# Modulation weights of a two-layer encoder: moved into the projection stage, through more buffers

## The reference

```python
def rwkv7_time_mix(h, prev_x, prev_wkv, p, l):
    shifted = jnp.concatenate([prev_x[:, None, :], h[:, :-1]], axis=1)
    xm = h[:, :, None, :] + (shifted - h)[:, :, None, :] * p['rw_mu'][l]
    rkv = jnp.einsum('bsnd,nde->bsne', xm[:, :, :3], p['rw_w_rkv'][l])      # the projection stage
    ...
    kk = kk * lax.rsqrt(jnp.maximum(jnp.sum(kk * kk, axis=-1, keepdims=True), 1e-24))
    ...
def run_trunk(x, c, ...):
    cs = jax.nn.silu(c)
    for l in range(DEPTH):
        mod = cs @ p['ada_w'][l] + p['ada_b'][l]                            # (1024) @ (1024, 6144)
        sh1, sc1, g1, sh2, sc2, g2 = jnp.split(mod, 6, axis=-1)
        ...
        h = modulate(rmsnorm(x, g), sh1, sc1); x = x + g1 * mixer(h)
        h = modulate(rmsnorm(x, g), sh2, sc2); x = x + g2 * hier_moe(h, p, l)
# shared_kv: one more such product, silu(c) @ kv_ada_w, (1024) @ (1024, 2048)
```

## Time and profile before

| | |
|---|---|
| Time, median of 3 runs | 1529.16 us |
| Lowest, highest | 1525.72 us, 1533.57 us |
| The profiled execution, span | 1526.5 us |
| TensorE (PE) busy | 1355.7 us, 89% of the span |
| VectorE (DVE) busy | 521.2 us, 34% |
| ScalarE (ACT) busy | 361.9 us, 24% |
| Read from HBM | 293.73 MB, mean 194 GB/s |

### The profile page before, as it was taken

One profiled execution on the slowest core, in us unless ns is written; L12 is line 12 of the kernel. 1 busy time (PEld: TensorE's weight loads), 2 busy tenths in 40 slices (PEclk: granted clock), 3 DMA queues, 4 the chain that ended last, 5 costly groups with the idle time before them and its releaser, 6 DMA issues.

```text
span 1526.5 us, 27571 instructions
## 1 busy us (share of the span) xinstructions
PE 1355.7 (89%) x11807; PEld 822.6 (54%) x11807; DVE 521.2 (34%) x1268; ACT 361.9 (24%) x664; POOL 68.4 (4%) x77
## 2 busy tenths in 40 slices
PE   5699998888888968999999996987968999999994
PEld 2257665565675655554444444656755555444443
DVE  2503553333312452332223235143262333222324
ACT  1131301110122022222222222134132222222212
POOL 2000000000000010000000000000010000000000
PEclk9799989998999875999999997996965999999997
DMA  9333216766734320888888845050220888888830
GB/s 272 92 111 120 100 62 244 285 234 237 276 113 165 111 83 1 331 324 299 305 304 299 305 186 184 11 205 17 83 83 1 331 330 320 302 307 298 302 121 34
DMA packets 111383, 297.16 MB, mean 195 GB/s; under 512 B 5924, under 2 KB 7304, under 8 KB 104136
## 3 DMA queue, kind: packets, MB, share of 16 engines
q1 hardware_dynamic: 109248, 289.78, 51.7%
q0 software_dynamic: 1856, 6.15, 1.7%
q10 hardware_dynamic: 200, 0.06, 0.0%
HBM read 293.73 MB, written 2.24 MB: 194 GB/s over the span
## 4 chain that ended last, share of the span: by engine, by line
PE 81%; DMA 8%; DVE 7%; ACT 2%; issue 1%; SPq 0%; DVEq 0%; POOL 0%; ACTq 0%; POOLq 0%
PE bank L664 79%; DMA ring<-in_ada_w 7%; DVE work L1415 3%; DMA ring<-in_kv_ada_w 1%; ACT work L1173 1%; PE bank L992 1%; DVE x_res L1421 1%; DVE work L1418 1%; DVE rstd L1453 1%; DVE att L1814 0%; PE bank L1159 0%; PE bank L1129 0%; PE bank L682 0%; SPq L450 0%; DVE work L1421 0%
## 5 line engine op out<-in xcount | busy, mean ns | idle before, releaser
L664 PE MATMUL bank<-work 128*128 128x128 bf16 (+6 forms) x3936 | 385.2, 255 | 20.0 <-ACT work L1173 7.4
L664 PEld LDWEIGHTS bank<-work 128*128 128x128 bf16 (+2 forms) x3936 | 282.1, 110 | 132.5 <-issue 30.6
L664 PE MATMUL bank<-ring,work 128*64 128x512 f32 (+1 forms) x1760 | 351.4, 553 | 1.5 <-DVE ring L1415 1.5
L664 PE MATMUL bank<-work,ring 128*128 128x320 f32 (+4 forms) x1600 | 298.9, 362 | 11.5 <-DVE work L1418 7.0
L664 PEld LDWEIGHTS bank<-work,ring 128*128 128x128 f32 (+3 forms) x1600 | 215.7, 171 | 96.2 <-issue 23.9
L664 PEld LDWEIGHTS bank<-ring,work 128*64 128x64 f32 (+1 forms) x1760 | 116.9, 138 | 214.1 <-issue 193.5
L664 PE MATMUL bank<-ring 64*64 64x64 f32 (+2 forms) x2624 | 110.7, 231 | 5.0 <-issue 5.0
L664 PEld LDWEIGHTS bank<-ring 64*64 64x64 f32 (+2 forms) x2624 | 97.5, 143 | 31.3 <-issue 25.1
L1173 ACT ACTIVATE work<-bank 64x512 f32<-64x512 f32 (+7 forms) x110 | 52.9, 528 | 226.1 <-PE bank L664 176.9
L664 PE MATMUL bank<-ring,cs 128*32 128x512 f32 x448 | 64.7, 671 | 38.6 <-DMA ring<-in_ada_w 34.4
L1762 DVE TENSOR_TENSOR work<-work,bank 128x320 f32<-128x320 f32 x128 | 62.4, 487 | 95.3 <-PE bank L664 95.3
(11 more groups left out here) (167 smaller groups left out, 879.9 us busy)
## 6 DMA issues: line engine op xcount, KB each, us to landing
ring<-in_moe_w_gu SPq DMA_DIRECT2D x64, 2048.0 KB, 12.9
ring<-in_moe_w_down SPq DMA_DIRECT2D x64, 1024.0 KB, 12.3
ring<-in_ada_w SPq DMA_DIRECT2D x40, 1024.0 KB, 5.1
ring<-in_rw_w_rkv SPq DMA_DIRECT2D x6, 2048.0 KB, 8.0
ring<-in_ada_w SPq DMA_DIRECT2D x4, 2048.0 KB, 31.5
ring<-in_kv_ada_w SPq DMA_DIRECT2D x8, 1024.0 KB, 5.0
ring<-in_rw_w_o SPq DMA_DIRECT2D x2, 2048.0 KB, 11.7
ring<-in_at_w_q SPq DMA_DIRECT2D x2, 2048.0 KB, 14.8
```

The lines of the kernel that those rows point to most:

```text
L664: return eng.matmul(out, l, r, start=start, stop=stop, **kw)
```

## The change

24 of the 48 steps move into the projection stage, one after each of its 24 output blocks (`project` gets an argument `step`). The chunk loop keeps two steps per chunk, and each level four, one after j = 0, 1, 2 and 4; as 48 steps are used up, level 5 has only two and level 6 none. Three buffers are used at first (steps 0 to 14), two for steps 15 to 23, three others from step 24 on (one of them shared). The weight loads of the projection are put between the pieces in SyncE's queue. Some small tiles move: `shiftT` and `modrow[0]` get places that are free in the projection stage, the load of `swin` waits for the last piece in its place, ScalarE waits for the shift output before it writes over `shiftT`, and for step 14 before it writes `vb` over a buffer. The two calls of `project` for n = 2 get `step=2 * C`, and the chunk loop on every engine goes over `steps_of_chunk(j)`.

```diff
-A_STEPS = 4
-LEVEL_STEPS = (2, 0, 2, 0, 2)
+P_STEPS = 24
+A_STEPS = 2
+LEVEL_STEPS = (1, 1, 1, 0, 1)
-    first = A_STEPS * NCH + sum(LEVEL_STEPS) * (l - 2)
+    first = P_STEPS + A_STEPS * NCH + sum(LEVEL_STEPS) * (l - 2)
+def steps_of_chunk(j):
+    return range(P_STEPS + A_STEPS * j, P_STEPS + A_STEPS * (j + 1))
+def mod_place(n):
+    if n < 15:
+        return n % 3
+    if n < P_STEPS:
+        return (n - 15) % 2
+    return (1, 3, 4)[(n - P_STEPS) % 3]
+def mod_before(n):
+    return max((k for k in range(n) if mod_place(k) == mod_place(n)), default=None)
+def mod_last(b):
+    return max(k for k in range(MSTEPS) if mod_place(k) == b)
...
-        shiftT = ring[:, tail1 + 1536:tail1 + 1792]
-        mw = [ring[:, 3 * B:3 * B + 2048], ring[:, tail3:tail3 + 2048]]
-        modrow = [ring[:, 3 * B + 2048:3 * B + 2560], work[:, 6 * B:6 * B + 512]]
+        shiftT = work[:, 7 * B:7 * B + 256]
+        mw = [ring[:, 4096:SLOT], ring[:, tail1:tail1 + 2048], work[:, 5 * B:5 * B + 2048],
+              ring[:, 3 * B:3 * B + 2048], ring[:, tail3:tail3 + 2048]]
+        modrow = [state[:, 1].rearrange("p c k -> p (c k)"), work[:, 6 * B:6 * B + 512]]
...
@@ SyncE's queue @@
-            for n in (1, 0, 2):
-                for hf in range(2):
-                    half(("rkv", n, hf), i["rw_w_rkv"][0, n], hf)
-            for n in range(MSTEPS):
+            def mod_load(n):
                 ...
-                if n >= 2:
-                    sp.wait("mod used", n - 2)
-                elif n == 1:
+                if mod_before(n) is not None:
+                    sp.wait("mod used", mod_before(n))
+                if n == P_STEPS + 1:
+                    sp.wait("used", "rkv", 2, 1)
+                if n == P_STEPS + 2:
                     sp.wait("bonus all", C - 1)
                 ...
+            for n in range(3):
+                mod_load(n)
+            for hf in range(2):
+                half(("rkv", 1, hf), i["rw_w_rkv"][0, 1], hf)
+            halves = {6: (0, 0), 10: (0, 1), 14: (2, 0), 17: (2, 1)}
+            for n in range(3, MSTEPS):
+                if n in halves:
+                    m, hf = halves[n]
+                    half(("rkv", m, hf), i["rw_w_rkv"][0, m], hf)
+                mod_load(n)
...
@@ GpSimd @@
-            pl.wait("wkv ready")
+            pl.wait("mod used", mod_last(1))
             eng.dma_start(swin, ...)
...
@@ TensorE @@
-            def project(tag, outs, src, wname, ready=None):
+            def project(tag, outs, src, wname, ready=None, step=None):
                     pe.did(ins, *keys)
+                    if step is not None:
+                        mod_step(step + m)
...
-                project(("rkv", n), range(C), xm[n], lambda hf, n=n: ("rkv", n, hf), ("xm", n))
+                project(("rkv", n), range(C), xm[n], lambda hf, n=n: ("rkv", n, hf), ("xm", n), step=C - C * n)
...
...
@@ ScalarE @@
             projected(1, kb, range(C))
+            mod_copy(range(0, C))
...
+            eng.wait_ge(in_sems["out_written"], 32)
             projected(0, rr, range(C))
+            mod_copy(range(C, 2 * C))
...
+            ac.wait("mod used", mod_last(2))
             projected(2, vb, range(4))
...
             projected(2, vb, range(4, C))
+            mod_copy(range(2 * C, 3 * C))
...
@@ VectorE @@
             ve.wait("xm used", 0)
+            mods_out(range(0, 2 * C))
...
             op(eng.tensor_copy(dend[:, :, :], dec[:, :, CH - 1:T:CH]))
+            mods_out(range(2 * C, 3 * C))
...
+            ve.wait("mod used", mod_last(0))
             for j in range(NCH):
```

More of the change, by code:

```diff
@@ L540, in _ @@
                 (ring[0:32, SLOT + 3072:SLOT + 4096], i["rw_g2"][0, P:LG])])
-            for n in (1, 0, 2):
-                for hf in range(2):
-                    half(("rkv", n, hf), i["rw_w_rkv"][0, n], hf)
-            for n in range(MSTEPS):
+            def mod_load(n):
                 w, l, blk, _b = MODS[n // C]
                 src = i[w] if l is None else i[w][l]
-                if n >= 2:
-                    sp.wait("mod used", n - 2)
-                elif n == 1:
-                    sp.wait("bonus all", C - 1)
-                else:
-                    sp.wait("used", "rkv", 2, 1)
-                eng.dma_start(mw[n % 2], src[P * (n % C):P * (n % C) + P, 2048 * blk:2048 * (blk + 1)]
-                              ).then_inc(in_sems[f"modw_in{n % 2}"], 16)
+                if mod_before(n) is not None:
[3 more added lines that the diff above has]
+                if n == P_STEPS + 2:
+                    sp.wait("bonus all", C - 1)
+                eng.dma_start(mw[mod_place(n)], src[P * (n % C):P * (n % C) + P, 2048 * blk:2048 * (blk + 1)]
+                              ).then_inc(in_sems[f"modw_in{mod_place(n)}"], 16)
+            for n in range(3):
[8 more added lines that the diff above has]
+                mod_load(n)
             sp.wait("mod used", MSTEPS - 1)
@@ L692, in mod_step @@
                         bank.hold("mod", g)
-                    eng.wait_ge(in_sems[f"modw_in{n % 2}"], 16 * (n // 2 + 1))
-                    pe.did(mod_rows(ps[seen_bank(("mod", g))], c, mw[n % 2]), ("mod used", n), ("mod", g))
+                    b = mod_place(n)
+                    eng.wait_ge(in_sems[f"modw_in{b}"], 16 * sum(mod_place(k) == b for k in range(n + 1)))
+                    pe.did(mod_rows(ps[seen_bank(("mod", g))], c, mw[b]), ("mod used", n), ("mod", g))
                 elif n == MSTEPS:
@@ L800, in _ @@
             head_sums("kk sum", nrm)
-            project(("rkv", 2), range(4), xm[2], lambda hf: ("rkv", 2, hf), ("xm", 2))
+            project(("rkv", 2), range(4), xm[2], lambda hf: ("rkv", 2, hf), ("xm", 2), step=2 * C)
             pe.wait("kk rstd")
@@ L805, in _ @@
             head_sums("bonus sum", tmp)
-            project(("rkv", 2), range(4, C), xm[2], lambda hf: ("rkv", 2, hf))
+            project(("rkv", 2), range(4, C), xm[2], lambda hf: ("rkv", 2, hf), step=2 * C)
             seen.at[("xm used", 2)] = (pe.name, pe.n)
@@ L832, in _ @@
                         full(ins, "A" + nm, j, hf)
-                for n in range(A_STEPS * j, A_STEPS * j + A_STEPS // 2):
+                for n in steps_of_chunk(j)[:A_STEPS // 2]:
                     mod_step(n)
@@ L843, in _ @@
                     full(ins, "tok" + nm, j)
-                for n in range(A_STEPS * j + A_STEPS // 2, A_STEPS * (j + 1)):
+                for n in steps_of_chunk(j)[A_STEPS // 2:]:
                     mod_step(n)
@@ L1249, in _ @@
                         ("read", "tok" + nm, j), ("tok ready", j))
-                mod_copy(range(A_STEPS * j, A_STEPS * (j + 1)))
+                mod_copy(steps_of_chunk(j))
             for l in range(2, 7):
@@ L1575, in _ @@
                 tt_(nl[:, :, t], nt[:, :, t], bmid(wcst("lev")[:, 64:128], C), M, ("level", 2, j))
-                mods_out(range(A_STEPS * j, A_STEPS * (j + 1)))
+                mods_out(steps_of_chunk(j))
                 ve.settle()
```

3 lines of the change are left out of this document (2 added, 1 removed).

## The result

The changed kernel takes 1492.21 us, the median of four runs (1489.34 to 1493.97), against 1527.44 us for the kernel before, measured beside it (four runs, 1520.86 to 1533.57). The ratio is 0.9759, with a 95% interval from 0.9725 to 0.9793. The forecast was 1491 us. The profiled execution has a span of 1492.2 us; it is the longest of the four, and its time was 1493.97 us.

A forecast was written before the change was run, and what follows sets the result against it. TensorE, 81% of the chain, was held in the loops by late weights and slow clock. Steps +4.1, waits -28.2 and clock -13.7 gave -37.8 on 1526.5, so 1488.7; plus 2.7, 1491 us (8 in 10: 1482 to 1506).

The forecast's parts named there:

- Waits for weights: Chunk and level loops: TensorE's 28.2 us of waits for modulation weights go, with 0 new waits taken.
- Clock: Chunk and level loops: 13.7 us of slow clock go back to the waits and vanish with them; at least 0.
- the work at full clock: Chunk and level loops without waits at full clock, all 48 steps included: 156.1 us, where the stretch took 202.3.
- Rival 2: Chunk and level loops: the waits go but the clock stays low, +13.7 us, 1505 us; chance 0.12.
- Steps in the projection: Projection stage: 24 added steps cost 1.15 us each, +27.6 us; bounds 0.93 to 1.61 each.
- Rival 1: Projection stage: each step drains the array, 1.61 us per step, +11 us, 1502 us; chance 0.13.
- an unseen cost per change of shape: Steps among full-array projection matmuls: a cost per array-shape change that no row shows, named the likeliest error; no size given.
- Steps out of the loops: Chunk and level loops: 24 steps leave, at 0.98 us each, -23.5 us.
- rival 3: Projection stage: DMA does not keep up and waits move there, ending slower, near 1550 us at 180 GB/s; chance 0.04.
- the milder form of this rival: Projection stage: at 240 GB/s DMA, steps 10, 14 and 17 wait some 9 us; 1500 us.
- Rival 4: Loops: they wait on something else, such as VectorE in the levels, turning 28 us of waits into others; chance 0.03.
- New waits: 0 new weight waits, at worst a few us; other engines cost nothing except up to 1 us for VectorE in level 6.

The follow-up runs named there:

- two_buffers_new_place: The changed kernel with two buffers at any time instead of three; 1492.48 us, ratio 0.9777.
- pieces_not_reloaded: The kernel before with only the first two weight pieces loaded and multiplied again by later steps, so results are wrong; 1481.95 us, ratio 0.9697.
- the two traffic kernels: The kernel before with weight loading kept up but no step waiting for it, in steady half-size or dense whole transfers; 1512.41 and 1486.14 us.
- pairs_in_projection: The changed kernel with two steps after every second projection block instead of one after each; 1486.99 us, ratio 0.9727.
- half pieces: The kernel before with three buffers and all steps in the old place, each piece loaded as two transfers of 1024 columns; 1510.44 us, ratio 0.9857.

## Why the prediction was right

It was right in the time (1491 against 1492.21 us), in both halves of the sum, and in their causes. That it came within 1.2 us is partly luck. It forecast a fall of 37.8 us; the medians fell by 35.2 and the profiled spans by 34.3. It started from a median of 1529.16 us for the kernel before, and the four runs beside the result have 1527.44, which hides 1.7 us of the difference. By its own terms:

- **Waits for weights, -28.2: right.** 28.2 before, none after. The cause was put down to supply in the chunks and spacing in the levels. `two_buffers_new_place` shows that the place is what does it: with half of the traffic gone from the loops, two buffers are enough.
- **Clock, -13.7: right in size, though the term holds more than clock.** `pieces_not_reloaded` gives back all 16.7, and the two traffic kernels show that it hung on the waits and not on the traffic. Apart from the first chunk's `A` groups the slow rows come to 12.3 us; some 4 us are the overlap lost at the waits, which the sum did not know. It did not show, as the work at full clock was put too high: 156.1 us, where `pieces_not_reloaded` has 153.8 without its slow `A` groups. 3.0 were set aside for those groups (6.61 us); in the changed kernel they take 5.38, so part of that came too. Rival 2, the clock staying low, falls: 0.97 and 1.00 in the loops.
- **Steps in the projection, +27.6 at 1.15 each: right.** A block and its step take 5.50 us where a block alone took 69.17 / 16 = 4.32: 1.18 a step, +28.3. With two turns (0.53 each) and a wait of 0.47, and 0.4 less elsewhere, that is the stretch's 29.4. Rival 1, the full drain at 1.61, falls: the price of a change there and back is 0.33 us, as `pairs_in_projection` shows. The Trainium skill has the rule that a change of tiling mode drains TensorE ("TensorEngine Tiling (Array Packing)", "Key Properties"). The trace agrees in so far as a change has a price; that this is a drain no run shows. The sentence that named an unseen cost per change of shape as the worst danger pointed at the right place; the cost was there and small.
- **Steps out of the loops, -23.5: a little too much.** In `pieces_not_reloaded` two steps back to back take 1.86 us from start to start (the 1.93 of the earlier trace rows holds the tail that overlaps what follows), and before nearly all were in pairs; the 24 that are left stand singly at 1.00. In all, the 48 steps of `pieces_not_reloaded` take 45.2 us and the 24 in the changed loops 23.9: -21.3.
- **DMA keeps up (rival 3): right.** No step waits in the projection at 223 GB/s on average, with 365 GB/s in one stretch of 8 us (100 to 108 us). The price of the milder form of this rival was mis-added: by the formula given there, 240 GB/s makes each cycle 4.3 us late, some 15 us in all, not 9.
- **Rival 4, another wait in place of the weights: falls.** In the loops PE waits for VectorE for 0.6 us, as before.
- **New waits: 0 for weights, and two small ones not foreseen.** `head_sums` waits 0.47 us, as it takes the bank that VectorE's `mods_out` has not finished reading. The "issue" gaps in the loops are 3.0 us instead of 1.3. Behind `s0` another 1.7 us are lost, where the sum had nothing: 0.4 in the longer gap of the recurrence and the rest in the slow clock behind it.

What the prediction had no idea of is that the same gains in another form are not the same. By its sum three buffers in the old place remove the same waits and the same clock loss and pay nothing in the projection: 28.2 - 2.7 = 25.5 us of waits and 13.7 of clock, for about 1487 us on the span. It took 1499.6. Of its 175.6 us in the loops, 156.1 are the work without loading; 9.5 are "issue" gaps and 2.7 weight waits; 7.2 are left. 3.0 of them are slow clock right behind the two longest gaps (0.69 from 317.58 to 323.00 us, 0.59 from 342.87 to 346.85), 0.5 lie in the first `A` groups, and 1.1 in a pair of steps that takes 3.03 us instead of 1.92 at a clock of 1.00; the rest is lost overlap. The gaps come of instruction packets that are late beside dense loading, where small matmuls use instructions up fast. The change keeps them at 3.0 us, as it moves half of the loading to a stage where PE takes few instructions: 650 records in 155 us, against some 3400 in 137 us of loops.

What stays open: what delays an instruction packet beside the weights, and why the second gap of the recurrence is 2.26 us in some kernels and 0.71 in others. Why the clock falls at some of the 16-row groups and not at others is open as well.

## What to carry to other kernels

Where a loop waits for its weights, look for a denser stage ahead of it that leaves the DMA queues idle: moved work costs there about what it did before (here 1.18 us a step for 0.93), and the loop gets back its waits and the time lost behind them, here 28.2 + 16.7 us. More buffers take the waits away but leave the loading dense; look then for "issue" gaps in the runs of small matmuls, and beside them for the packets of the instruction queue. Put moved pieces of another array shape together in pairs where the stream around is of full-array matmuls, and singly where they pace a buffer's reloading.

## What the runs showed of the hardware that was not expected

- Loading at 345 to 357 GB/s beside 64 x 64 float32 matmuls opens gaps of 0.2 to 1.5 us in TensorE's work (4.0 us in 37); at 229 GB/s there are 0.2 us in 157 in the same loops, and none without loading. Where three pieces go round in the loops, gaps are up to 2.6 us long, with half pieces up to 4.2.
- These gaps go with late instructions. Instructions come in packets of 16 KB, one for 128 matmul records on average, and in 79 gaps of 79 TensorE starts again 1.2 to 1.6 us after a packet has ended. Under the dense loading nine such packets started 68 records later on average than without it.
- Going from 128 x 128 tiles to 128 x 32 tiles and back costs 0.33 us for float32.
- TensorE's clock fell behind waits and gaps of 2.2 to 3.0 us in a stream that was otherwise busy. Behind the wait of 2.67 us it was 0.64 from 321.11 to 326.81 us, and 128 records took 5.77 us instead of 3.95. It stayed full at the same traffic without them. It also fell over a spread that uses 16 rows with PE busy all along: 0.68 from 213.40 to 219.97 us, 6.63 us for 16 records, where the other spread of the same kernel took 4.57 at a clock of 1.00.
